# The first MLP's gate and up products by seven half-token products, its down products in 4 by 4 blocks

## The reference

```python
f = rms_norm(h, ffn_pre_norm[i])
f = (jax.nn.silu(f @ w_gate[i]) * (f @ w_up[i])) @ w_down[i]
h = h + rms_norm(f, ffn_post_norm[i])
```

## Time and profile before

| | |
|---|---|
| median of 3 runs | 1989.74 us (1988.11 to 1991.95) |
| time of the profiled execution | 1993.29 us |
| its span, first to last instruction | 1991.5 us |
| mean granted PE clock | 0.98 |
| PE, PEld busy | 96%, 85% |
| DVE, ACT, POOL busy | 64%, 39%, 8% |
| DMA, mean over the span | 84 GB/s |

### The profile page before, as it was taken

The page is one execution under the profiler, slowest core; times in us unless marked ns, Lnnn a source line. Parts: engine busy times, 40 slices in busy tenths (PEclk is TensorE's granted clock), DMA queues, the critical chain, the costliest instruction groups (busy, mean ns, idle before and its releaser), DMA issues.

```text
span 1991.5 us, 28681 instructions
## 1 busy us (share of the span) xinstructions
PE 1910.0 (96%) x11702; PEld 1685.0 (85%) x11702; DVE 1279.4 (64%) x1912; ACT 784.2 (39%) x1180; POOL 156.8 (8%) x127
## 2 busy tenths in 40 slices
PE   7999899999999999999998999999899989999996
PEld 6876777888888778899888999999899868998995
DVE  7676736434434676667658877776555469777764
ACT  4555524212213353444435444443322245444441
POOL 3000023000000220000012000000300030000001
PEclk9999999999999999999998999999999989999998
DMA  5130121232222321111111322323122312322321
GB/s 180 64 105 22 54 66 67 101 101 90 96 95 85 106 85 64 43 43 65 60 48 64 106 88 104 106 86 106 64 85 85 107 64 85 108 104 97 104 96 43
DMA packets 26077, 166.44 MB, mean 84 GB/s; under 512 B 3808, under 2 KB 4064, under 8 KB 6624
## 3 DMA queue, kind: packets, MB, share of 16 engines
q1 hardware_dynamic: 25232, 163.52, 23.9%
q10 hardware_dynamic: 720, 1.14, 0.2%
HBM read 162.55 MB, written 2.10 MB: 83 GB/s over the span
## 4 chain that ended last, share of the span: by engine, by line
PE 86%; DVE 10%; ACT 2%; issue 2%; DMA 0%; POOL 0%; SPq 0%; ACTq 0%; DVEq 0%
PE ps L373 13%; PE ps L374 13%; PE ps L375 13%; PE ps L2526 6%; PE ps L2527 6%; PE ps L2528 6%; PE ps L2542 4%; PE ps L2541 4%; PE ps L2540 4%; PE ps L2295 2%; PE ps L2296 2%; PE ps L2297 2%; DVE ps L530 2%; DVE h L543 2%; PE ps L2349 1%
## 5 line engine op out<-in xcount | busy, mean ns | idle before, releaser
L373 PE MATMUL ps<-z_hi,w_hi 128*128 128x512 f32 (+1 forms) x1008 | 369.0, 366 | 31.3 <-DVE z_lo L481 28.1
L374 PE MATMUL ps<-z_lo,w_hi 128*128 128x512 f32 (+1 forms) x1008 | 365.0, 362 | 0.0
L375 PE MATMUL ps<-z_hi,w_lo 128*128 128x512 f32 (+1 forms) x1008 | 363.3, 360 | 0.0
L355 DVE TENSOR_TENSOR w_lo<-w_raw,w_hi 128x2048 fp32r<-128x2048 f32 x95 | 217.8, 2293 | 89.8 <-ACT w_hi L344 89.7
L373 PEld LDWEIGHTS ps<-z_hi,w_hi 128*128 128x128 f32 x1008 | 195.0, 193 | 68.9 <-issue 22.8
L2526 PE MATMUL ps<-arena,w_hi 128*128 128x256 f32 (+2 forms) x768 | 245.6, 320 | 0.5 <-DVE acc L1857 0.5
L2527 PE MATMUL ps<-arena,w_hi 128*128 128x256 f32 (+2 forms) x768 | 246.0, 320 | 0.0
L2528 PE MATMUL ps<-arena,w_lo 128*128 128x256 f32 (+2 forms) x768 | 245.4, 320 | 0.0
L344 ACT ACTIVATE w_hi<-w_raw 128x2048 fp32r<-128x2048 f32 x95 | 181.0, 1905 | 147.7 <-PE ps L375 134.9
L375 PEld LDWEIGHTS ps<-z_hi,w_lo 128*128 128x128 f32 x1008 | 195.0, 193 | 30.1
L374 PEld LDWEIGHTS ps<-z_lo,w_hi 128*128 128x128 f32 x1008 | 195.2, 194 | 29.0 <-issue 0.7
(11 more groups left out here) (357 smaller groups left out, 4148.9 us busy)
## 6 DMA issues: line engine op xcount, KB each, us to landing
w_raw<-wstream SPq DMA_DIRECT2D x151, 1024.0 KB, 4.8
out<-h SPq DMA_DIRECT2D x8, 256.0 KB, 2.0
w_raw<-wstream SPq DMA_DIRECT2D x2, 512.0 KB, 6.1
h<-xT ACTq DMA_DIRECT2D x4, 256.0 KB, 6.7
h<-xT SPq DMA_DIRECT2D x4, 256.0 KB, 6.3
rope_cs<-pT SPq DMA_DIRECT2D x1, 512.0 KB, 5.5
acc<-pos SPq DMA_DIRECT2D x1, 256.0 KB, 10.4
acc<-lam SPq DMA_DIRECT2D x1, 128.0 KB, 9.8
```

The costliest lines, as they stand in the source:

```text
L355: dve.tensor_tensor(w_lo[:, slot, :], w_raw[:, slot, :], w_hi[:, slot, :].bitcast(f32), ALU.subtract).then_inc(wlo, 1)
L373: pe.matmul(dst, wh, zh, start=(k == 0), stop=False)
L374: pe.matmul(dst, wh, zl, start=False, stop=False)
L375: last = pe.matmul(dst, wl, zh, start=False, stop=(k == nk - 1))
```

## The change

- `FIRST1 = 5`: the first 5 gate-up blocks stay. The other 17 are made of seven products (`g_seven`) with 4 k-tiles each and 256 of 512 tokens.
- The down products come in 12 blocks of 4 output tiles (`fall`): ten of 4 k-tiles (48 matmuls of 512 columns), two of 2 k-tiles (24 each, half a weight block). Block `fall(q)` stands before the gate-up pair 5+2q, 6+2q. `acc` gets 48 additions instead of 24, the first 8 of them copies, so POOL's zeroing goes.
- Sums and differences of token halves are made once, during the first 5 blocks, in `acc` and `arena`; per seven-product block there are four sums of weights, made in `rr`, `sq` and in place in `w_raw`.
- The up branch is no longer multiplied by `R1`. The norm behind the MLP makes this good: its epsilon is replaced by a term per token (`e_col`), for which PE makes 4 more one-column matmuls in `g_stat`.
- POOL clears the part of `arena` after the sums of squares of the MLP's output instead of before the MLP.
- The second and third MLP change only in semaphore counts. The stream has as many weight blocks as before, in another order.

```diff
+DOWNS1 = 12
 FF2 = 4096 // P
 NCH2 = FF2 // KD
 DIFF_HEADS = 8
...
+def gate_block(i):
+
+    return i if i < FIRST1 else FIRST1 + 3 * ((i - FIRST1) // 2) + 1 + (i - FIRST1) % 2
+
+
+def fall_block(q):
+
+    return FIRST1 + 3 * q if q < 9 else FF1 + q
+
+
+def fall_tiles(q):
+
+    return 4 if q < DOWNS1 - 2 else 2
...
-            once(dve, "col_part", pi + 1, dve.tensor_copy(total, ps[:, col_bank, 0:n]))
+            if pi == 1:
+                dve.wait_ge(e_col, 1)
+                once(dve, "col_part", pi + 1, dve.tensor_tensor(total, cols[:, U_COL:U_COL + n], ps[:, col_bank, 0:n], ALU.add))
+            else:
+                once(dve, "col_part", pi + 1, dve.tensor_copy(total, ps[:, col_bank, 0:n]))
...
@@ -728,12 +762,8 @@
             pool_sum(pool, 1, S, META)
             pool_sum(pool, 2, S, META)
 
-            def zero_acc(pi):
-                pool.wait_ge(resid, 8 * pi + 8)
-                pool.memset(acc[:, :], 0.0).then_inc(acc_zero, 1)
-            zero_acc(0)
+            pool_sum(pool, 3, S, META)
             pool.memset(arena[:, A_2 + 8 * T:ARENA].bitcast(f32), 0.0).then_inc(s("pv_zero"), 1)
-            pool_sum(pool, 3, S, META)
 
             pool.wait_ge(s("a_max"), 16)
             pool.iota(dist[:, :], pattern=[[1, T]], base=-(S - P + META), channel_multiplier=-1,
...
+            def g_keep(i, j):
+                b, n = B_MLP1 + gate_block(i), i - FIRST1
+                slot = (P_MLP1 + gate_block(i)) % 2
+                if j < 3:
+                    act.wait_ge(s("e_prod"), since("e_prod", 5 * n + (1, 2, 4)[j]))
+                else:
+                    act.wait_ge(ps_full, 2 * pair_of(b) + 2)
+                act.activation(kept(j, S), ps[:, 4 * slot + (0, 1, 0, 0)[j], 0:256], ACT.Copy).then_inc(s("e_kept"), 1)
...
+            def gate_in(i):
+                if i < FIRST1:
+                    p = pair_of(B_MLP1 + gate_block(i))
+                    dve.wait_ge(ps_full, 2 * p + 1)
+                    dve.wait_ge(s("sw_silu"), i)
+                    dve.tensor_tensor(tt(0, S), banks(p % 2, 0, S), R1, ALU.mult).then_inc(ps_free, 1)
+                else:
+                    n = i - FIRST1
+                    dve.wait_ge(s("e_y"), since("e_y", 2 * n + 1))
+                    dve.wait_ge(ps_free, 2 * pair_of(B_MLP1 + gate_block(i)) + 1)
+                    dve.tensor_tensor(tt(0, S), tt(0, S), R1, ALU.mult).then_inc(s("e_g"), 1)
+
+            def gated(i):
+                p = pair_of(B_MLP1 + gate_block(i))
+                dve.wait_ge(s("sw_silu"), i + 1)
+                dve.wait_ge(s("sw_hi"), i)
+                if i < FIRST1:
+                    dve.wait_ge(ps_full, 2 * p + 2)
+                    last = dve.tensor_tensor(tt(3, S), banks(p % 2, 1, S), tt(2, S), ALU.mult)
+                    last.then_inc(ps_free, 1)
+                    dve.wait_ge(ps_free, 2 * p + 2)
+                    dve.sem_inc(s("sw_hm"), 1)
+                else:
+                    dve.wait_ge(s("e_y"), since("e_y", 2 * (i - FIRST1) + 2))
+                    dve.wait_ge(ps_free, 2 * p + 2)
+                    dve.scalar_tensor_tensor(tt(3, S), tt(1, S), -1.0, tt(2, S), op0=ALU.mult, op1=ALU.mult).then_inc(s("sw_hm"), 1)
+
...
+            def g_sum(i, j):
+                b, n = B_MLP1 + gate_block(i), i - FIRST1
+                slot = b % 2
+                a11, a12, a21, a22 = (w_raw[:, slot, 512 * x:512 * x + 512] for x in range(4))
+                e1, e2, e4 = E_RAW1[0], E_RAW1[1][:, 0:512], E_RAW1[1][:, 512:1024]
+                if j == 0:
+                    dve.wait_ge(raw_in[slot], 16 * (b // 2 + 1))
+                else:
+                    dve.wait_ge(s("e_sum"), since("e_sum", 4 * n + j))
+                out, x, y = [(e1, a21, a22), (e2, e1, a11), (e4, e2, a12), (a21, a21, a11)][j]
+                dve.tensor_tensor(out, x, y, ALU.add).then_inc(s("e_sum"), 1)
+
+            def g_factor_low(i, part):
+                n = i - FIRST1
+                dve.wait_ge(s("e_hi"), since("e_hi", 2 * n + part + 1))
+                a, e = [(0, 512), (512, 1536)][part]
+                dve.tensor_tensor(e_part(1, a, e), E_RAW1[part], e_part(0, a, e).bitcast(f32), ALU.subtract).then_inc(s("e_lo"), 1)
+
...
+            def g_quarter(i, j):
+                n = i - FIRST1
+                p, slot = pair_of(B_MLP1 + gate_block(i)), (P_MLP1 + gate_block(i)) % 2
+                bank_u, bank_b, bank_a, bank_d = (ps[:, 4 * slot + x, 0:256] for x in range(4))
+                if j == 0:
+                    dve.wait_ge(s("e_prod"), since("e_prod", 5 * n + 3))
+                    dve.wait_ge(s("e_kept"), since("e_kept", 4 * n + 1))
+                    dve.wait_ge(s("sw_silu"), i)
+                    dve.tensor_tensor(tt(0)[:, 0:256], bank_a, kept(0, S), ALU.add).then_inc(s("e_y"), 1)
+                elif j == 1:
+                    dve.wait_ge(ps_full, 2 * p + 1)
+                    dve.wait_ge(s("e_kept"), since("e_kept", 4 * n + 3))
+                    dve.tensor_tensor(tt(0)[:, 256:512], bank_b, kept(2, S), ALU.add).then_inc(ps_free, 1)
+                elif j == 2:
+                    dve.wait_ge(s("e_prod"), since("e_prod", 5 * n + 5))
+                    dve.wait_ge(s("e_kept"), since("e_kept", 4 * n + 4))
+                    dve.wait_ge(s("sw_hm"), i)
+                    dve.tensor_tensor(tt(1)[:, 0:256], bank_d, kept(3, S), ALU.add).then_inc(s("e_y"), 1)
+                else:
+                    dve.tensor_tensor(tt(1)[:, 256:512], bank_u, kept(1, S), ALU.add).then_inc(ps_free, 1)
+
...
+            def fall(q, t):
+                b = B_MLP1 + fall_block(q)
+                n, slot = 2 * pair_of(b) + t, (P_MLP1 + fall_block(q)) % 2
+                dve.wait_ge(ps_full, n + 1)
+                dst, src = ac(4 * (q % 2) + t)[:, META:T], ps[:, 4 * slot + 2 * (t % 2), :]
+                if q < 2:
+                    dve.tensor_copy(dst, src).then_inc(ps_free, 1)
+                else:
+                    dve.wait_ge(ps_free, n)
+                    dve.tensor_tensor(dst, dst, src, ALU.add).then_inc(ps_free, 1)
+            gt1, gt2, gt3, gt4 = (t_raw(j, S).rearrange("p (a b) -> p a b", a=4) for j in range(4))
+            g_early, g_late = slice(META, META + 256), slice(META + 256, T)
+            gg = [smc(GAIN[1][0], GAIN[1][1] + k) for k in range(KD)]
...
+                a, b = FIRST1 + 2 * q, FIRST1 + 2 * q + 1
+                if q:
+                    g_quarter(a - 1, 2)
+                    g_quarter(a - 1, 3)
+                else:
+                    dve.wait_ge(s("t_lo"), since("t_lo", 4))
+                    gate_in(a - 1)
+                g_sum(a, 0)
+                g_sum(a, 1)
+                gated(a - 1)
+                g_sum(a, 2)
+                g_sum(a, 3)
+                fall(q, 0)
+                g_factor_low(a, 0)
+                gated_low(a - 1)
+                fall(q, 1)
+                g_factor_low(a, 1)
+                g_weight_low(gate_block(a))
+                fall(q, 2)
+                fall(q, 3)
+                if q < 8:
+                    for j in range(4):
+                        g_sum(b, j)
+                else:
+                    g_weight_low(fall_block(9))
+                g_quarter(a, 0)
+                if q < 8:
+                    g_factor_low(b, 0)
+                    g_weight_low(gate_block(b))
+                g_quarter(a, 1)
+                gate_in(a)
+                if q < 8:
+                    g_factor_low(b, 1)
+                    g_quarter(a, 2)
...
+                    gated(a)
+                    gated_low(a)
+                    g_quarter(b, 0)
+                    g_weight_low(fall_block(q + 1))
+                    g_quarter(b, 1)
+                    gate_in(b)
+            g_quarter(FF1 - 1, 2)
+            g_quarter(FF1 - 1, 3)
+            gated(FF1 - 1)
+            fall(9, 0)
+            gated_low(FF1 - 1)
+            short_low(10)
+            fall(9, 1)
+            for k in range(2):
+                dve.wait_ge(s("p_hi"), k + 1)
+                dve.tensor_tensor(a_ple(1, k), rope_cs[:, k, :], a_ple(0, k).bitcast(f32), ALU.subtract).then_inc(s("p_lo"), 1)
+            fall(9, 2)
+            fall(9, 3)
+            fall(10, 0)
+            short_low(11)
+            for t in range(1, 4):
+                fall(10, t)
+            fall(11, 0)
+            fall(11, 1)
+            dve_lo(dve, B_PLEP, B_PLEP % 2)
+            fall(11, 2)
+            fall(11, 3)
 
...
+            def g_stat():
+                slot = P_MLP1 % 2
+                pe.wait_ge(summed, summed_to(2))
+                pe_columns(pe, ps[:, 4 * slot + 3, 0:4], [ssum[:, META:T]], S)
+                pe_stat(pe, 2, slot, S, META)
+
...
+            def fall(q):
+                b, c, nk = B_MLP1 + fall_block(q), q // 2, fall_tiles(q)
+                p, slot = pair_of(b), (P_MLP1 + fall_block(q)) % 2
+                pe.wait_ge(wlo, b + 1)
+                pe.wait_ge(s("sw_lo"), 4 * c + nk)
```

(49 more changed lines are left out.)

289 lines of the change are left out of this document (198 added, 91 removed).

## The result

| | before | after the change |
|---|---|---|
| median of the runs, us | 1990.85 (1988.11 to 1993.30) | 1972.03 (1970.86 to 1974.43) |
| the profiled execution, and its span | 1993.29, 1991.5 | 1971.16, 1969.4 |

The ratio is 0.9907, 95% interval 0.989 to 0.9925: 18.8 us faster between the medians. The predicted time was 1971.4.

What follows compares the result with a forecast made beforehand. PE was taken to bound the kernel, busy 96% of the span. -19.2 + 0.5 + 0.4 = -18.3 us takes the profiled 1993.29 to 1975.0; less 3.6 above the median, 1971.4 us is expected, range 1967 to 1980.

Steps and rivals of the forecast that it cites:

- -19.2 us for seventeen blocks: First MLP: each seven-product block spares PE 1.13 us against a plain gate-up block; 17 blocks, 19.2 us less.
- +0.5 for the one-column matmuls: Four more one-column matmuls on PE, priced from a row where 24 take 2.89 us: +0.5 us.
- +0.4 at the end: End of the first MLP: DVE's split ends at 11.5 us, PE wants it at 11.1; +0.4, between 0 and 1.
- rival 1: Small PE waits in each pair, 0.35 to 1.5 us, take 3 to 13 us of the gain; chance 0.16.
- The walk: One pair's DVE operations laid out against PE's needs: first down addition 0.24 us to spare, split 0.6; no waits.
- DVE's 26.5 us in a pair: DVE's summed work per pair in the first MLP: 26.5 us of PE's 31.1, 85%, so it fits.
- 0 for leaving out `R1`: Dropping 17 and more DVE multiplications that stood beside PE's work changes the time by 0.
- 0 at the start: Start of the first MLP: 4.6 us of DVE token sums in a 3.77 gap cost 0 to 0.3; 0 taken.
- 0 for POOL's memset: POOL's memset of 6.05 us, moved behind the last sum of squares, is covered by 34 us of nothing: 0.
- Rival 2: DVE sets the pace; slower once PE waits over 2.0 us per pair, 1998 at 3 us; chance with rival 3 0.05.
- rival 3: PE's waits also cost clock, seen after 3.55 us idle; not under a microsecond; chance with rival 2 0.05.
- Rival 4: Weight loads do not hide behind 256 columns in the first MLP: 80 us more, 2070 us; chance 0.03.

Runs made afterwards that it cites:

- n22_order: The change with all 22 gate-up blocks left plain, the first down addition ahead of the split; stage 388.4 us against 369.3, ratio 1.0009 to the kernel before.
- pad_one: The change plus one independent DVE multiplication of 512 columns just ahead of the first down addition of each pair; ratio 0.993 to the kernel before.
- r1_back: The change with the multiplication by R1 put back on the hidden tile of every gate-up block; ratio 0.993 to the kernel before.
- n22_plain: The change with all 22 gate-up blocks left plain, but a DVE split ahead of the first down addition; ratio 1.0083 to the kernel before.
- pad_four: The change plus four DVE multiplications ahead of the split of each pair's first gate-up block; ratio 1.0045 to the kernel before.
- pad_split: The change plus three dependent DVE multiplications ahead of the split of each pair's first gate-up block; ratio 0.9975 to the kernel before.

## Why the prediction was right, and where its terms were off

- **-19.2 us for seventeen blocks.** n22_order against the change gives 19.1. The third MLP's rows were the right price: the distances of 10.00 and 11.14 us came back in the new place.
- **+0.5 for the one-column matmuls.** Mis-sized: they took 0.9 us. The price came from a row with "x24", 2.89 us, and it was counted as 24 matmuls. The trace has eight records for the four that are added here, so by the same price of 0.12 us each it should have been 8 x 0.12 = 0.96.
- **+0.4 at the end.** The wait for the projection's split was 0.39 us. With 0.9 it makes the 1.3 us that the kernel with the new order and no seven-product block took more than before. -19.1 + 0.9 + 0.4 = -17.8 us is the whole difference of the stage. The 18.8 us between the medians are a little more, and that they came so near to the forecast of 18.3 is in part luck: the terms of the sum give 17.8.
- **0 for the waits in a pair (rival 1).** The walk held to 0.1 us at every step that was named, and PE does not wait. That the 0.24 us were real spare, and all there was, is shown by pad_one and r1_back: with 0.61 and 0.74 us put ahead of the addition PE waits at once.
- **DVE's 26.5 us in a pair.** It was 25.0. The order of the operations, and not this sum, decides, as n22_plain shows.
- **0 for leaving out `R1`.** This term was badly put. "Beside PE's work" is true of the time of DVE, but one of those multiplications stands ahead of the addition that PE waits for. Put back, it costs 4.9 us. The walk had counted without it and so came out right; as a part by itself it is worth a quarter of the gain.
- **0 at the start.** Right in sum for another reason than laid out. The difference took 2.31 us beside POOL instead of 1.22, the eight small ones 0.29 us each instead of up to 0.42.
- **0 for POOL's memset.** Right: 24 us of nothing remain behind it.
- **Rival 2, its turning point.** I had it at 2.0 us of wait in each pair, and 3 us a pair at 1998. As long as the clock stays, 2.0 is right: 17.8 / 9, where the wait is what a pair gets longer by (2.31 us where the profile shows 2.06). pad_four is past it by its waits alone, 20 us, and the clock adds 6: it is 0.45% slower than before. But the clock is missing from the rival's times. The step that failed is "it is counted in rival 2": the clock behind each wait was named in rival 3 and never priced. At 3.5 us it costs 2.4 us on top of 3.6, and the kernel takes 2028.45; at 2.06 it costs 1.5 us in four of the pairs; at 1.3 nothing. Rival 3's "waits of under a microsecond do not reach this" is borne out by r1_back, pad_one and even pad_split.
- **Rival 4, the loads.** They do hide behind 256 columns. But the floor is at 111 ns and the products stand at 119, 7% above it. The prediction's break-even of 132 ns was one way to see the margin; how near the next halving is to being worthless it did not see. The figures of the Trainium skill that the prediction set against its own ("TensorE: Matmul & The Clock Gate", section "Back-to-back issue gap": 81 ns at 128 columns, 131 at 512) are too low for this kernel at both ends, where it has 111 and 232; the measurement decides.
- **The profiled execution.** It stood 3.6 us above the median before, and I took that off. That fits the clock of 0.77 in its window 40 to 60 us, and the first landmark 6.0 us later than in the changed kernel.

No version was found that beats the change. What is left of PE's waits between 308 and 651 us comes to the 0.39 us at the end, and the one attempt on it made it worse.

## What to carry to other kernels

Price a transplanted block from the rows of a stage that has it already, then lay out one period of the engine that serves the bottleneck, instruction by instruction, against the moment at which each bank and each weight is wanted. Put first what the bottleneck wants next, not what could be started soonest: a split ahead of an addition cost as much as four fifths of this change's gain. A bank or a split that comes late costs its lateness and 0.1 to 0.2 us more (0.16 in pad_one, 0.13 in pad_split). The lower clock can come on top: never behind the waits of 1.3 us here, behind four of eight waits of 2.06 us, and behind every one of 3.5. Look at the distance of the next matmuls to see whether it came. And count a price per record as the trace counts records, not as the program counts instructions.

## What the runs showed of the hardware that I had not expected

- **A floor of 111 ns for a matmul that loads its own 128x128 fp32r weights.** At a clock of 1.00: 232 ns at 512 columns, 119 at 256, 111 at 128 and at 64. Cutting columns below 256 wins 7% per matmul here, and below 128 nothing. At the lower clock the floor was 213 ns.
- **The clock can fall with PE shown busy throughout.** At 64 columns the granted clock stood at 0.50 between 380 and 400 us; at 128 and 256 columns it stayed at 1.00 there (one execution each of the two narrow kernels).
- **A wait of the same length does not cost the same each time.** 2.06 us in pad_four: clock 0.95 in one pair, 1.00 in the next.
- **A one-column matmul of `pe_columns` stands in the trace as two records.** Four of them are the "x8" at 311.90, which took 0.81 us to the next start.
- **A sum on POOL lengthens what DVE does beside it** by 1.0 to 1.1 us while it runs for 1.33: a subtraction of two SBUF tiles, but also four `tensor_scalar` with one SBUF tile (0.29 us each alone). The Trainium skill ("SBUF — State Buffer", section "Who interferes with whom") has an instruction with two SBUF inputs contend with a reading GpSimd, and `tensor_scalar` when it runs in a mode with two ports; both fit these rows, though no row says in which mode the copies ran. DVE's additions from PSUM beside the same kind of sum (L577, 0.68 us) were not longer.
